# Convolution sums in PSUM, new first queues, scales by logarithm and exponential, and gate groups between the last down projections

## What is computed

```python
h = rms(x, g_mix)                       # x / sqrt(mean(x^2) + eps) * g
z = h @ w_in                            # 1024 -> 2048 columns: b | c | v | u, 512 each
hc = c * v
conv = w0*hc[t-2] + w1*hc[t-1] + w2*hc[t]          # depthwise, per channel
a = b * conv
d = trailing_mean_w(u) - u              # w = 2, 4, 8, 16 in four groups of 128 channels
bb = blockdiag(d, w_pool) * pool_scale
x = x + concat(a, bb) @ w_out           # 1024 -> 1024
f = relu(rms(x, g_mlp) @ w_up)          # 1024 -> 4096
x = x + (f * f) @ w_down                # 4096 -> 1024
x = x + (p @ w_ple) * sigmoid(rms(x, g_ple) @ w_ple_gate)
y = rms(x, g_final)                     # and the last 2 rows of hc, last 15 of u
```

## Time and profile before

| what | us |
|---|---|
| median of 3 runs (lowest, highest) | 796.15 (781.3, 796.78) |
| the profiled execution | 780.77 |
| its span, slowest core (core 2) | 779.2 |
| PE busy | 727.5 |
| DVE busy | 572.4 |
| ACT busy | 302.7 |
| POOL busy | 234.0 |

### The profile page before, as it was taken

How to read it: one execution, slowest core, us unless ns; L and a number is a source line. 1 busy time by engine, 2 the same in 40 slices (tenths; PEclk the granted TensorE clock), 3 DMA queues, 4 the chain that set the end, 5 groups by cost and what they waited for, 6 DMA issues and landing times.

```text
span 779.2 us, 12661 instructions; the slowest of 8 cores (777.4 to 779.2 us)
## 1 busy us (share of the span) xinstructions
PE 727.5 (93%) x3996; PEld 397.9 (51%) x3996; DVE 572.4 (73%) x927; ACT 302.7 (39%) x506; POOL 234.0 (30%) x247
## 2 busy tenths in 40 slices
PE   2898997999999999999999999999999999999862
PEld 0444554555555555555555555555555555555431
DVE  3688799788956766666566567667887896787876
ACT  3455645364572122112111218533433433633442
POOL 1566464657612000000000002024233423334223
PEclk9999999899999999999999999999999999999986
DMA  8995000006339533344333344425456972686222
GB/s 200 180 197 201 1 1 0 1 1 109 61 62 154 102 55 55 61 75 81 56 55 56 54 75 75 75 49 84 85 148 122 158 138 63 108 163 119 44 80 88
DMA packets 13393, 68.04 MB, mean 87 GB/s; under 512 B 1680, under 2 KB 3600, under 8 KB 8080
## 3 DMA queue, kind: packets, MB, share of 16 engines
q0 software_dynamic: 8064, 49.96, 37.9%
q1 hardware_dynamic: 5120, 17.18, 6.3%
q10 hardware_dynamic: 144, 0.09, 0.1%
HBM read 108.59 MB, written 8.59 MB: 150 GB/s over the span
## 4 chain that ended last, share of the span: by engine, by line
PE 81%; DVE 6%; issue 5%; DMA 3%; POOL 2%; ACT 2%; DVEq 0%; POOLq 0%; ACTq 0%
PE ps L725 28%; PE ps L737 28%; PE ps L608 8%; PE ps L754 7%; PE ps L699 6%; DMA arena<-w_in 3%; PE ps L747 2%; DVE arena L551 2%; PE ps L564 1%; PE ps L535 1%; POOL arena L640 1%; DVE arena L671 1%; ACT arena L472 1%; DVE arena L679 1%; POOL arena L501 0%
## 5 line engine op out<-in xcount | busy, mean ns | idle before, releaser
L693 DVE TENSOR_TENSOR arena<-arena,ps 128x416 f32<-128x416 f32 x360 | 207.6, 584 | 41.1 <-PE ps L699 10.5
L737 PE MATMUL ps<-arena 128*128 128x416 bf16 x1280 | 235.7, 339 | 0.0
L725 PE MATMUL ps<-arena 128*128 128x416 bf16 x1280 | 231.7, 339 | 0.0
L730 ACT ACTIVATE arena<-arena 128x416 bf16<-128x416 f32 x160 | 86.6, 548 | 234.0 <-DVE arena L728 232.3
L725 PEld LDWEIGHTS ps<-arena 128*128 128x128 bf16 x1280 | 125.1, 98 | 101.4 <-issue 2.8
L737 PEld LDWEIGHTS ps<-arena 128*128 128x128 bf16 x1280 | 125.2, 98 | 100.9 <-issue 1.6
L728 DVE SCALAR_TENSOR_TENSOR arena<-ps,arena 128x416 f32<-128x416 f32 x160 | 93.9, 587 | 86.5 <-PE ps L725 76.0
L608 PE MATMUL ps<-arena 128*128 128x416 bf16 (+1 forms) x640 | 129.9, 355 | 23.8 <-DMA arena<-w_in 17.5
L608 PEld LDWEIGHTS ps<-arena 128*128 128x128 bf16 x640 | 64.4, 101 | 83.3 <-issue 38.6
L501 POOL TENSOR_TENSOR arena<-arena 128x416 f32<-128x416 f32 (+1 forms) x47 | 69.1, 1470 | 66.5 <-ACT arena L494 52.4
L472 ACT ACTIVATE arena<-arena 128x416 bf16<-128x416 f32 (+1 forms) x120 | 72.0, 634 | 25.5 <-DVE arena L693 13.5
(11 more groups left out here) (65 smaller groups left out, 451.4 us busy)
## 6 DMA issues: line engine op xcount, KB each, us to landing
arena<-w_up POOLq DMA_DIRECT2D x19, 1024.0 KB, 10.1
arena<-w_down POOLq DMA_DIRECT2D x19, 1024.0 KB, 9.6
yt<-arena SPq DMA_DIRECT2D x20, 416.0 KB, 3.6
arena<-xt SPq DMA_DIRECT2D x8, 832.0 KB, 11.7
arena<-w_in POOLq DMA_DIRECT2D x8, 512.0 KB, 12.9
arena<-w_out POOLq DMA_DIRECT2D x2, 1024.0 KB, 16.2
arena<-w_gate POOLq DMA_DIRECT2D x1, 2048.0 KB, 16.7
arena<-xt SPq DMA_DIRECT2D x2, 864.0 KB, 10.2
```

The source lines that it names most:

```text
L693: pg.op("dve", lambda e: e.tensor_tensor(out=xs(t, d), in0=xs(t, d), in1=PS[b][:, 0:TN], op=ALU.add), c_dve(TN), reads=[("ps", b), ("x", t ...
L725: pg.op("pe", [lambda e, k=k: e.matmul(PS[b][:, 0:TN], lhsT=UPB[j % 2][:, k, c * 128:(c + 1) * 128], rhs=hs(t, k), start=(k == 0), stop=(k ...
L730: pg.op("act", lambda e: e.activation(out=FT[w % NFT][:, c, :], in_=TMP[rs], func=AF.Square), c_act(TN), reads=[("tmp", rs)], writes=[("fT ...
L737: pg.op("pe", [lambda e, i=i, j=j, w=w, k=k: e.matmul(PS[b][:, 0:TN], lhsT=DNB[j % 2][:, k, d * 128:(d + 1) * 128], rhs=FT[w % NFT][:, k, ...
```

## The change

Seven things change; tile sizes do not (the new table TS holds five times 416).

1. The convolution's accumulator is a PSUM bank (6 or 7): one tap on ACT, the two others and the product with the scale on DVE. Banks 6 and 7 are kept out of the rotation until the w_in stage is over.
2. root is a logarithm and an exponential with factor -0.5, both on ACT, in place of square root and reciprocal; the division by 1,024 has gone into the ones matrix.
3. First queues: SP loads the constants, then x of tile 0 in quarters; POOL loads w_in chunk 0 after the first quarter and all others behind it without waits; x of tile 1 comes after chunk 1 has landed, tiles 2 to 4 after the first half of w_out. The sum of squares of tile 0 is made in quarters, by four fp32 matmuls, with 14 matmuls between them whose result is not used. More groups of tile 0 (ten) come before the first of tile 1 (two).
4. The adds of the input norm's squares are on POOL alone. The norms' work has other places: N1 of the next tile earlier, N2 of tiles 0 and 1 in tile 4's w_in stage, N2 of tile 2 in the MLP, N2 of tiles 3 and 4 just before these tiles start. Only three buffers hold the MLP scales.
5. Buffers lie elsewhere: H of tile 0 and the temporaries now lie over the w_in stage's buffers (S, vS, U, hcv), and the MLP starts with tile 1.
6. The last down projection of tile 4 has x's gain, its squares and the gate matmuls of three groups, chunk by chunk, between its groups; the last norm sums chunk squares by eight fp32 matmuls, writes one copy of the scale to PSUM for DVE and one to SBUF for POOL, and stores the last two chunks singly.
7. The planner reckons DMA landings from a model of shared queues and makes five passes, not three.

```diff
+    ACCB = 6
+    bankrot, kept = [0], {ACCB, ACCB + 1}
...
-            adders = ("dve",) if fast else ("pool", "dve")
+            adders = "pool" if self.full else ("pool", "dve")
...
         def root(self, b):
-            pg.op("act", lambda e: e.activation(out=rt, in_=PS[b][:, 0:n], func=AF.Sqrt, bias=epsb[:, 0:1], scale=1.0 / D),
-                  c_acts(n), reads=[("ps", b), ("epsb",)], writes=[rk], table="sqrt")
-            for a in range(0, n, q):
-                pg.op("dve", lambda e, a=a: e.reciprocal(out=rt[:, a:min(a + q, n)], in_=rt[:, a:min(a + q, n)]), 0.06 + 0.0065 * q,
+            pg.op("act", lambda e: e.activation(out=rt, in_=PS[b][:, 0:n], func=AF.Ln, bias=epsb[:, 0:1]),
+                  c_acts(n), reads=[("ps", b), ("epsb",)], writes=[rk], table="exp")
+            pg.op("act", lambda e: e.activation(out=rt, in_=rt, func=AF.Exp, scale=-0.5), c_acts(n), reads=[rk], writes=[rk], table="exp")
...
+        def finish(self, b, pooled):
+            for k in pooled:
+                pg.op("act", lambda e, k=k: e.activation(out=xs(t, k), in_=xs(t, k), func=AF.Copy, scale=gcol[:, g, k:k + 1]),
...
+            pg.op("act", lambda e: e.activation(out=rt, in_=PS[b][:, 0:n], func=AF.Ln, bias=epsb[:, 0:1]),
+            pg.op("act", lambda e: e.activation(out=PS[b][:, 0:n], in_=rt, func=AF.Exp, scale=-0.5), c_acts(n),
+            pg.op("act", lambda e: e.activation(out=rt, in_=rt, func=AF.Exp, scale=-0.5), c_acts(n), reads=[rk], writes=[rk], table="exp")
+                if k in pooled:
+                    pg.op("pool", lambda e, k=k: e.tensor_tensor(out=xs(t, k), in0=xs(t, k), in1=rt, op=ALU.mult),
+                else:
+                    pg.op("dve", lambda e, k=k: e.scalar_tensor_tensor(out=xs(t, k), in0=xs(t, k), scalar=gcol[:, g, k:k + 1],
+                                                                       in1=PS[b][:, 0:n], op0=ALU.mult, op1=ALU.mult),
...
+            ab = ACCB + slot
+            acc = PS[ab][:, mo:mo + n]
+            pg.op("act", lambda e: e.activation(out=acc, in_=C.hcv[:, c, 0:n], func=AF.Copy, scale=ccol[:, c:c + 1]),
+            for tap in (1, 2):
+                pg.op("dve", lambda e, tap=tap: e.scalar_tensor_tensor(
+                    out=acc, in0=C.hcv[:, c, tap:tap + n], scalar=ccol[:, 4 * tap + c:4 * tap + c + 1], in1=acc, op0=ALU.mult, op1=ALU.add),
+            pg.op("dve", lambda e: e.tensor_tensor(out=C.acc[:, slot, 0:n], in0=acc, in1=N.rt[:, z0:z0 + n], op=ALU.mult), c_dve(n),
...
+    xq = [pg.dma("sp", lambda e, q=q: e.dma_start(out=X[0][:, 2 * q:2 * q + 2, :],
...
+    wq = [loadwin(h, [xq[0]] if h == 0 else ()) for h in range(8)]
...
+    x1 = loadx(1, [wq[1]])
+    loadx(4, loadx(3, loadx(2, [wo[0]])))
...
+    N1[0].quarter(sb, 0)
+    idle(0, 6)
+    N1[0].quarter(sb, 1)
+    idle(2, 8)
+    held = zhold(0, 0, 1)
+    N1[0].quarter(sb, 2)
+    N1[0].quarter(sb, 3)
+    N1[0].end(sb)
...
-    a0 = up(0, 0)
+    N2[2].pre()
+    a1 = up(0, 1)
     for c in range(4):
         pmgroup(L, c)
-    a1 = up(0, 1)
+    a0 = up(0, 0)
+    N2[2].S()
...
-    down([prev[0]], prev[1])
-    N3[4].xg()
...
+    for d in range(KD):
+        dgroup([prev[0]], 4, d)
+        N.xg((d,))
+        N.chunk(d, 5)
+        if d >= 2:
+            part(d - 2)
+    part(6)
+    N.onesum(sb, 0, True, False)
+    N.onesum(sb, 6, False, False)
+    part(7)
+    N.onesum(sb, 7, False, True)
+    N.known(sb)
...
+    for d in range(G, 6):
+        hold4(d)
+    N, sb = NL[4], None
+    for d in range(KD):
+        cev(4, d, (cple(4, d), held[d]), inps=d >= 6, load=N.load if d == 7 else None)
+        if d < 2:
+            hold4(6 + d)
+        N.square(d, ("act", "pool") if d < 4 else ("act",) if d < 6 else ("pool",) if d == 6 else ("dve",))
+        if d >= 4:
+            N.onesum(sb, d - 4, d == 4, False)
+    for k in range(4, KD):
+        N.onesum(sb, k, False, k == 7)
+    N.finish(sb, (1, 3, 5))
```

More of the change, by code:

```diff
@@ L193, in _pass @@
             end = start + cost + 0.1
-            if n.dma:
+            if n.dma and n.i in self.landing:
+                end = start + cost + self.landing[n.i]
+            elif n.dma:
                 wire = max(wire, start + cost) + n.flight
@@ L339, in build_program @@
     per = Bump(0, ARENA_BYTES)
-    W = [TW0] + [TN] * (NT - 1)
+    W = [TW0] + list(TS[1:])
     X = []
@@ L366, in build_program @@
     RM = []
-    for t in range(NT):
-        o = per.take(TN * 4); RM.append(vf32(o, TN)); pg.place(("rm", t), o, TN * 4)
+    for t in range(3):
+        o = per.take(TS[t] * 4); RM.append(vf32(o, TS[t])); pg.place(("rm", t), o, TS[t] * 4)
     wout_o = per.take(16384)
@@ L566, in S @@
-            self.root(b, 2 if self.g < 2 else 4)
-            if self.full:
-                i = rtrot[0] % 4
-                rtrot[0] += 1
-                r2, r2k = RT[i][:, 0:n], ("rt", i)
-                self.r2, self.r2k = r2, r2k
-                pg.op("act", lambda e: e.activation(out=r2, in_=rt, func=AF.Square), c_act(n), reads=[rk], writes=[r2k])
+            pg.op("pe", lambda e: e.matmul(PS[b][:, 0:n], lhsT=ones, rhs=self.src, start=True, stop=True), 4 * c_pe(n),
+                  reads=[("ones",), self.sk], writes=[("ps", b)])
```

513 lines of the change are left out of this document (286 added, 227 removed).

## The result

The changed kernel takes 757.2 us (median of four runs, 756.6 to 757.7) where the kernel before takes 781.5 (seven runs, 780.4 to 781.9) on the same chip: ratio 0.969, 95% interval 0.968 to 0.971. The first measurement gave the same ratio, 0.969 (0.966 to 0.973), with a median of 757.98 us. The forecast was 749.2 us, range 738 to 766. In some executions, whatever the kernel, the cores of one die show a lower clock and take longer (in the first measurement one of four, 875.57 us); they are left out of the ratios.

A forecast was written before the change was run, and what follows sets the result against it. TensorE was taken as nearly full mid-kernel and thin at both ends, with VectorE the bound late in the w_in stage; gains 6 + 9.8 + 1.3 + 14.5 = 31.6 us turn 780.77 into 749.2 us, range 738 to 766.

The forecast's parts named there:

- Front: Start to 59.07 us: new load queues and order bring the first 22 w_in groups 6 us earlier, bounds 2 to 10.
- the text's 52.5: Start of the kernel: forecast time in us when 22 w_in groups and four pooling matmuls are done, against 59.07 before.
- rival 1: Start of the kernel: no earlier, w_in limited by the wires, x1 only waits longer; loses 6 us, 756 us; 12%.
- w_in stage: 59.07 to 205.32 us: VectorE relieved by PSUM taps and no reciprocals, gain 9.8 us, bounds 0 and 12.
- 3 of the 13 us: w_in/w_out stages: TensorE loses 13 us of 146.25 before the change; 3 were forecast to remain, gain 9.8.
- rival 5: w_in stage: slower, six banks too few, each TensorE stop costs 6.8 us, ten stops give 817 us; 2%.
- rival 2: w_in stage: VectorE or the banks go on holding TensorE, taps at 0.87 us; loses the 9.8, 759 us; 10%.
- MLP: 205.32 to 727.26 us: TensorE already full, about 1.8 us lost; 1.3 us gained back, bounds -3 to 1.8.
- Tail: From 727.26 us to the end: gate parts between the last down projections, gain 14.5 us, bounds 8 to 16.
- 9.2 plus 0.8 of the text: End of the kernel: last scale, products and store after TensorE ends at 754.7, to 763.9, with 0.8 us more allowed.
- TensorE's walk: From the last down projection: TensorE's 27.4 us of work runs without idling, from 727.26 to 754.7 us.
- Rivals 3 and 4: Logarithm and exponential in two tables, 757 us, 6%; last tile's VectorE or ScalarE chain late, TensorE idles, 756 us, 6%.

## Why the prediction was right, and where it was not

The direction, "faster", and the range held; the gain was 31.6 us by the sum and 22.4 by the trace. Three terms were too large, one too small. The range was also added up wrong: the terms' best bounds are 10, 12, 1.8 and 16 us, 39.8 together, which gives 741 us and not 738.

- **Front: -6 forecast, +1.2 measured on the slowest core; the step that failed is the landing of x of tile 1.** (At the start of the first w_out group, in the mean of eight cores, the change gains 1.3 us, 61.1 to 59.8; the 2.90 us before it were counted to the next stage.) The first quarter of x landed at 7.1 us instead of 5.1, and chunk 0 let TensorE start at 16.27 (forecast 13.8). Chunk 3 landed at 26.6 us (forecast 28), chunk 4 at 32.4 (31), chunks 5 to 7 at 37.0, 40.7 and 43.8 (34, 37, 40); in the kernel before the last three landed at 36.4, 40.9 and 43.5 (core 2). They came no earlier, which is the condition that the text gave its lower bound of 2 us, and x of tile 1 came 10 us later than before. It was put at 28 us, with two chunks beside it. It was requested at 18.9 and landed at 36.0 us: 17.1 us for 1,664 KB, in which more than three chunks went by. Its price was nearly right: by the trace's DMA packets its queue had 0.31 of the engines' time in that stretch, 5.3 us of all engines where 4.9 was summed. Its share was wrong, for the software queue had 0.70.

  By TensorE's timeline, ten groups of tile 0 were done at 37.1 us instead of 34.0 (a wait of 2.72 us for chunk 4, and a granted clock of 0.50 behind it); then TensorE stood 2.69 us for tile 1, and 16 matmuls at half clock cost 1.7 more. That is 7.5 of the 7.8 us between the text's 52.5 and 60.27. This is rival 1, at 12%, with its own reason, "x1 only waits longer", and its 756 us is nearer to what was measured than the forecast's 749. The experiment with the old queues shows the step from the other side: with x of tile 1 requested at once, among the other old requests, the 22 groups are done 4 us earlier. What the new queues bring in its place, ScalarE's copies no longer behind the squares of tile 2, was no term of the sum. The experiment with tile 0 first gets 1.9 us back.
- **w_in stage: -9.8 forecast, -14.05 measured (0.7 of it the sum that moved out).** I kept 3 of the 13 us as lost; none is. The price of the taps was a little low: 648 ns for a tap that reads SBUF and PSUM and writes PSUM, 583 for the product, against 584 for all. VectorE's share of 79% is within the forecast 75 to 85. What was wrong is the weight of the parts. I counted the reciprocals as half of VectorE's relief (5.8 of 11.1 us); with them back and the taps in PSUM no stop returns. With the taps in SBUF and no reciprocal, two stops return on every core. So the place of the taps is what counts, and the rows point at the long instructions that meet GpSimd, 1.5 to 2.2 us each, not at the sum of busy time. Six banks in place of eight cost 1.1 us in that case (3.3 against 2.2 us of stops), and in the changed kernel, with six banks, TensorE has no stop in this stage, so rival 5 had no place, nor rival 2.
- **MLP: -1.3 forecast, +2.4 measured (+1.7 without the moved sum).** The text named "new waits at the start of up" with buffers of the pooling stage as what would be wrong. It was the start of up, but another buffer: that of the state stores. VectorE waited there before too, 2.3 us, with no effect on TensorE; in the changed kernel it waits 6.6 us and TensorE 2.05 us, with the slow clock behind it. I had not followed the state copies into the new order of work. With a buffer for each store the MLP takes 520.46 us on every core, 1.5 less than before with the moved sum in it, so the rest of the term held.
- **Tail: -14.5 forecast, -12.0 measured.** From the last matmul to the end 10.1 us passed, the 9.2 plus 0.8 of the text. The term that was mis-sized is TensorE's walk, 27.4 us of pure work. It took 29.9 (716.83 to 746.74): 0.23 us for an activation, 0.80 for a sum of squares on GpSimd (L577), 0.45 for a square (L595), and 1.0 us for which no row names a releaser, part of it the ends of matmuls, which run past the distance of starts. "TensorE never idles" fails by 1.5 us of named waits; "without a gap over 1 us" holds.
- **Rivals 3 and 4** did not come: Ln and Exp share a table (eleven table loads in all, none between the two), and the last tile's chain holds TensorE for no more than 0.8 us at a time. By the Trainium skill, "ScalarE: Activation LUTs", section "Table sets: the hidden batching unit", one set holds both functions; the trace agrees (746.84 and 747.54 us, 0.70 us apart). By the Trainium skill, "SBUF — State Buffer", section "Who interferes with whom", an instruction of VectorE with two SBUF inputs contends with one of GpSimd that reads SBUF; the trace agrees, with 1.45 against 0.59 us for the same sum.

So the range held partly by luck: the front, forecast at 6 us, gave next to nothing, and the w_in stage gave 4 us more than its term.

What stays open: why one core of a pair ends later than the other in the changed kernel, and what sets the share of each of the two queues. In the first profiled execution the first work on x starts at 7.0 to 7.2 us on the late core of each pair and at 5.3 to 6.2 on the other, the first w_out group starts 1.3 to 2.7 us later on it, and the stop for the state store takes 1.3 to 2.0 us against 0.3 to 0.7; that is where the difference enters, not why. Six banks against eight were not compared with the taps in PSUM, and the new queues were not tried with x of tile 1 requested at once.

## What to carry over

Look for the instructions that become long when two engines meet in SBUF, and for what waits behind them: with three instructions per block on PSUM a stage has no stop at VectorE 86% busy, with the taps in SBUF it has two at 81%. When a stage gets denser, follow every small shared buffer and every in-order queue across it again: a store's landing that was covered before (2.3 us of VectorE's time) held TensorE afterwards, and copies in ScalarE's order behind work that waits for a load held it for 4.4 us in the mean with the old queues. And a transfer that shares its engines with a full software queue lets everything pass that stands there, not only the chunks meant to go first: x needed 17.1 us where I had summed 11.1. Last, compare stages by the mean of the cores as well as by the slowest: the slowest one had lost 3.7 us in a stop that cost four of the others 0.3 to 0.7.

## What was not expected of the hardware

- SP's transfer beside a full software queue: 1,664 KB in 17.1 us, 100 KB/us, with 0.31 of the engines' time against 0.70 for the software queue (116 KB/us). The price of 350 KB/us that the page gives for SP's queue is per us of all engines' time. x of tile 0, with the software queue still empty, came at only 179 KB/us at 2.0 to 7.7 us, with 0.94 of the engines' time.
- Eight matmuls at half of their rate (3.04 us against 1.62) behind 4.1 us of idle time, while the windows view reads 1.00, since the clock record has no entry yet.
- A stop of 2.05 us in full work was followed by a granted clock of 0.50 on core 1, stops of 1.3 to 1.5 us on cores 3, 5 and 7 of the same execution were not.
- The landing of a small state store: its buffer was free 9.4 us after the copy in the changed kernel, over 13 us after it in the kernel with half of w_in. In the changed kernel it landed 0.15 us behind a block of w_down that had been requested 0.9 us before it (202.67 and 202.52 us), in the kernel before 0.2 us behind one (220.42 and 220.22), with half of w_in 2.9 us behind one. What it waits for is not shown.
- Products on GpSimd of 416 columns take 1.03 us each in the last row (3.10 for three) while VectorE reads its scale from PSUM, and 1.40 (4.20 for three) while VectorE reads both inputs from SBUF.
